# Grouping two matmuls with the rounded weights and two with their remainder in the experts' gate and up products

## What is computed

```python
gate, idx = lax.top_k(aff.T, cap)
xg = xt[idx]
h = jax.nn.silu(jnp.einsum('ecd,edf->ecf', xg, w_gate)) * jnp.einsum('ecd,edf->ecf', xg, w_up)
y = jnp.einsum('ecf,efd->ecd', h, w_down) * gate[..., None].astype(x.dtype)
out = jnp.zeros_like(xt).at[idx.reshape(-1)].add(y.reshape(-1, D))
```

## Time and profile before

| | |
|---|---|
| median of 3 runs | 1766.36 us (1766.05 to 1768.7) |
| the profiled execution: its time | 1767.66 us |
| the profiled execution: first to last instruction (span) | 1765.8 us |
| mean granted TensorE clock | 0.988 of full speed |
| PE matmul, busy | 1717.8 us (97%) |
| PE weight loads, busy | 1554.8 us (88%) |
| DVE, busy | 1192.7 us (68%) |
| ACT, busy | 1074.2 us (61%) |
| POOL, busy | 391.2 us (22%) |

### The profile page before, as it was taken

One profiled execution on the slowest core, in us unless ns is written; L12 is line 12 of the kernel. 1 busy time (PEld: TensorE's weight loads), 2 busy tenths in 40 slices (PEclk: granted clock), 3 DMA queues, 4 the chain that ended last, 5 costly groups with the idle time before them and its releaser, 6 DMA issues.

```text
span 1765.8 us, 30625 instructions
## 1 busy us (share of the span) xinstructions
PE 1717.8 (97%) x10812; PEld 1554.8 (88%) x10812; DVE 1192.7 (68%) x2367; ACT 1074.2 (61%) x2140; POOL 391.2 (22%) x552
## 2 busy tenths in 40 slices
PE   9999999899999989998999999999999999999994
PEld 9789898788888878887999999999999999999994
DVE  4442533488888972147777877787777877778776
ACT  4333333389999983332566756667666666666665
POOL 1322402255555542220110011100110011100112
PEclk9999999899999999998999999999999999999998
DMA  7556645665545742334786787867868678676885
GB/s 237 129 164 196 193 127 152 161 168 156 150 150 145 217 114 107 114 114 166 266 269 247 256 263 237 273 237 256 273 227 274 240 263 279 220 265 251 268 274 220
DMA packets 203488, 367.18 MB, mean 208 GB/s; under 512 B 39055, under 2 KB 64655, under 8 KB 202831
## 3 DMA queue, kind: packets, MB, share of 16 engines
q1 hardware_dynamic: 190268, 320.92, 54.3%
q0 software_dynamic: 13120, 44.96, 9.9%
HBM read 321.67 MB, written 50.45 MB: 211 GB/s over the span
## 4 chain that ended last, share of the span: by engine, by line
PE 48%; DVE 2%; DMA 2%; ACT 1%; POOL 1%; issue 0%; DVEq 0%; SPq 0%; ACTq 0%; POOLq 0%
PE psum L2148 21%; PE psum L2150 10%; PE psum L2167 3%; PE psum L2168 3%; PE psum L2169 3%; PE psum L2170 3%; PE psum L2171 3%; PE psum L2133 1%; DMA own_rows<-x 1%; DMA x<-y_s,index 0%; DVE raw_weights L1848 0%; DMA rows_s<-xn,tokens 0%; DVE weight_parts L1781 0%; ACT xT_e L2012 0%; POOL final_stats L1740 0%
## 5 line engine op out<-in xcount | busy, mean ns | idle before, releaser
L2148 PE MATMUL psum<-x_parts,weight_parts 128*128 128x384 f32 x2048 | 583.6, 359 | 0.0
L2150 PE MATMUL psum<-x_parts,weight_parts 128*128 128x192 f32 x2048 | 512.7, 250 | 0.0
L1781 DVE TENSOR_TENSOR weight_parts<-raw_weights,weight_parts 128x1024 fp32r<-128x1024 f32 x384 | 451.4, 1220 | 69.3 <-ACT weight_parts L1980 69.3
L1980 ACT ACTIVATE weight_parts<-raw_weights 128x1024 fp32r<-128x1024 f32 x384 | 381.8, 1055 | 23.5 <-DMA raw_weights<-in_w_gate 11.0
L2150 PEld LDWEIGHTS psum<-x_parts,weight_parts 128*128 128x128 f32 x2048 | 391.2, 191 | 0.6
L2148 PEld LDWEIGHTS psum<-x_parts,weight_parts 128*128 128x128 f32 x2048 | 384.4, 188 | 0.8
L603 PE MATMUL psum<-x_hi,w_parts 128*128 128x512 f32 x624 | 193.6, 390 | 0.0
L1721 POOL DMA_INDIRECT x<-y_p,index x15 | 24.1, 1609 | 640.4 <-DVE y_s L1843 640.4
L2007 ACT ACTIVATE h_parts<-up_sum 128x192 fp32r<-128x192 f32 x128 | 46.7, 365 | 169.8 <-DVE up_sum L1796 169.6
L1212 PE MATMUL psum<-w_o_parts,mixed_parts 128*128 128x512 f32 x576 | 140.8, 397 | 1.2 <-DVE w_o_parts L1349 1.2
L603 PEld LDWEIGHTS psum<-x_hi,w_parts 128*128 128x128 f32 x624 | 117.1, 188 | 26.9 <-issue 2.6
(11 more groups left out here) (221 smaller groups left out, 3127.9 us busy)
## 6 DMA issues: line engine op xcount, KB each, us to landing
raw_weights<-in_w_gate SPq DMA_DIRECT2D x32, 2048.0 KB, 7.8
raw_weights<-in_w_up SPq DMA_DIRECT2D x32, 2048.0 KB, 8.6
raw_weights<-in_w_down SPq DMA_DIRECT2D x32, 2048.0 KB, 8.9
mixed<-in_w_in SPq DMA_DIRECT2D x96, 256.0 KB, 4.3
q_parts<-q SPq DMA_DIRECT2D x188, 128.0 KB, 3.1
bias_da<-da_rows SPq DMA_DIRECT2D x31, 512.0 KB, 4.4
q<-mixed POOLq DMA_DIRECT2D x96, 128.0 KB, 3.1
mixed<-in_x SPq DMA_DIRECT2D x12, 512.0 KB, 6.9
```

What stands on the lines that cost most here:

```text
L1781: dve.tensor_tensor(part_half(u, 1, half), src, part_half(u, 0, half).bitcast(F32), ALU.subtract).then_inc(split, 1)
L1980: act.activation(part_half(u, 0, half), src, ACT.Copy).then_inc(rounded, 1)
L2148: pe.matmul(out.rearrange("p (h n) -> p h n", h=2), w[:, 0, k, cols], x_parts[:, k, :, :], start=(k == 0), stop=False)
L2150: mm = pe.matmul(out[:, 0:SLOTS], w[:, 1, k, cols], x_parts[:, k, 0, :], start=False, stop=(k == KT - 1))
```

## The change

In `product` the loop over the 8 feature tiles k becomes a loop over 4 pairs of tiles. In each pair the two hi matmuls stand together, then the two lo matmuls. The instructions are the same, with the same operands; the wait for the second half of the first expert's tokens (`x_split`) stays ahead of k = 4.

```diff
-                    for k in range(KT):
-                        if k == HALF_KT and second_half:
+                    for pair in range(0, KT, 2):
+                        if pair == HALF_KT and second_half:
                             pe.wait_ge(x_split, second_half)
-                        pe.matmul(out.rearrange("p (h n) -> p h n", h=2), w[:, 0, k, cols], x_parts[:, k, :, :],
-                                  start=(k == 0), stop=False)
-                        mm = pe.matmul(out[:, 0:SLOTS], w[:, 1, k, cols], x_parts[:, k, 0, :],
-                                       start=False, stop=(k == KT - 1))
+                        for k in (pair, pair + 1):
+                            pe.matmul(out.rearrange("p (h n) -> p h n", h=2), w[:, 0, k, cols], x_parts[:, k, :, :],
+                                      start=(k == 0), stop=False)
+                        for k in (pair, pair + 1):
+                            mm = pe.matmul(out[:, 0:SLOTS], w[:, 1, k, cols], x_parts[:, k, 0, :],
+                                           start=False, stop=(k == KT - 1))
                     return mm
```

## The result

The changed kernel takes a median of 1771.72 us over 20 runs (1769.63 to 1774.54), the kernel before in the same series 1767.72 us (1765.46 to 1769.78): a ratio of **1.0023, 95% interval 1.0017 to 1.0029, 4.0 us slower**. The forecast was 1765.4 us in a range of 1761 to 1770, with 0.07 for slower.

The account below looks back on a forecast made before the run. TensorE's own pace was taken to bound the experts. A group of two hi and two lo was to stay at 568.8 ns; with 1.0 us taken off for the kernel, the forecast was 1765.4 us, range 1761 to 1770.

Parts of the forecast that it names:

- the rival with loads further ahead: In TensorE, the second lo's load is done beneath the second hi; 35.2 ns saved a group, 1730.4 us; chance 0.03.
- The rival with neighbours at their own pace: Two lo in a row step at 93.3 ns; 17.6 ns saved a group, 1748.4 us; chance 0.06.
- no step falls below 110 to 112 ns: In TensorE, one weight load sets a minimum step of 110 to 112 ns, whether 128 columns pass or 16.
- the list for each group: For hi, hi, lo, lo: 173.5, 173.5, 110.9 and 110.9 ns, in sum 568.8, the same as before.
- the order cannot matter: Each matmul in a product covers one equally wide load, so a group takes 568.8 ns in either order.
- The bounds: Time of a group hi, hi, lo, lo: 564.0 to 570.6 ns, or 4.9 us less to 1.8 us more.
- The rival that ended on the other side: Two late loads in a row delay the next hi; 1024 groups lose 20 us, 1787 us; chance 0.07.
- point of decision: Loss per group from which the slower rival counts: 3.4 ns, or 3.5 us (about 0.2%) for the kernel.
- the 16-column run: The router's 16-column matmuls; the first 512-column one after them takes 0.25 us against 0.227, some 0.02 us lost.

Follow-up runs that it names:

- e8: Changed order with lo narrowed from 192 to 128 columns; median 1769.03 us, ratio to before 1.0008.
- e2: Changed order with lo widened from 192 to 256 columns; median 1791.73 us, ratio to before 1.0139.
- e15: Changed kernel, but each expert's first gate product alternates hi and lo as before; median 1765.04 us, ratio to before 0.9989.
- e3: Changed order, but the lo of odd k adds to the second half of the bank; median 1771.41 us, ratio to before 1.0024.
- e5: Alternating order of before with lo widened to hi's 384 columns; median 1893.69 us, ratio to before 1.0717.
- e6: Changed order with lo widened to hi's 384 columns; median 1894.57 us, ratio to before 1.0715.
- e10: Alternating order of before with one group hi, hi, lo, lo at the start of each product; median 1775.59 us, ratio to before 1.0050.
- e13: Alternating order of before with one group hi, hi, lo, lo per expert, in its first gate product; median 1776.79 us, ratio to before 1.0057.
- e14: Alternating order of before, only the first lo of each expert has 256 columns; median 1767.53 us, ratio to before 1.0003.
- e7: Order of before, but each product has one place with two hi and one with two lo, apart; median 1770.17 us, ratio to before 1.0017.
- e4: Each product runs its eight hi, then its eight lo, where before alternates; median 1772.01 us, ratio to before 1.0027.
- e9: Order of before, but each product has two hi in a row mid-product and two lo at its end; median 1775.13 us, ratio to before 1.0043.
- e1: Alternating order of before with lo widened from 192 to 256 columns; median 1785.67 us, ratio to before 1.0108.
- e12: Changed order with lo widened from 192 to 320 columns; median 1848.43 us, ratio to before 1.0463.
- e11: Alternating order of before with lo widened from 192 to 320 columns; median 1845.38 us, ratio to before 1.0444.

## Why the prediction was wrong

**What held.** TensorE's own pace was the only thing that counted; no wait, no other engine and no transfer had a part in it. The load sets the lo step, and only one set of weights is loaded ahead: in the groups every load starts 2 ns or more after the matmul ahead of it, none two matmuls early, and e8's shorter lo holds the array no less. So the rival with loads further ahead fell. The Trainium skill, "TensorE: Matmul & The Clock Gate", section "Back-to-back issue gap", gives a sustained 81 ns for 128 columns and 131 ns for 512. This case does not agree: a lo of 128 columns takes 108 to 112 ns in the changed order too (e8). The rival with neighbours at their own pace fell as well; two lo in a row take 108.3 and 110.9 ns. One reading was too wide, though without effect on the sum: that no step falls below 110 to 112 ns. The transposes behind expert 8, also of 128 columns, stand in the trace of before as

```profile
1335.56 0.80 PE L2133 MATMUL psum<-ident_r,rows_p 128*128 128x128 f32 x8
1336.19 0.46 PE L2167 MATMUL psum<-weight_parts,h_parts 128*128 128x512 f32 x1
```

that is eight steps in 0.63 us, 79 ns each. The floor belongs to the loads of the products, not to every load of 128 columns.

**The step that failed** is the list for each group, two hi of 173.5 ns and two lo of 110.9, with its conclusion that the order cannot matter. Measured, the four are 179.9, 174.3, 108.3 and 110.9 ns: 573.4 in place of 568.8, and the mis-sized term is the first hi. It took a step's length for a property of the step and its neighbour, so that lengths read in other runs could be added up. The runs show that the length of a hi step depends on how the sequence was entered: 176.1, or 179 and 184 ns by turns, in one and the same alternation, 179.9 and 174.3 or 176.6 and 170.8 in one and the same group order. The bounds fell with it: 564.0 to 570.6 ns a group were put together from steps of other sequences, and hold the fast pace (566.6) but not the slow one (573.4) in which the change runs.

**The rival that ended on the other side** had the place right: the first hi after two lo went from 176.1 to 179.9 ns, in record from 358 to 362, and the loss of 4.5 ns a group is above its point of decision, 3.4. Its mechanism was not: it made the lateness of two loads the debt and priced it at 20 us from the 16-column run. The debt comes without late loads (e2), does not grow with them (e8), and is absent in e15 with the same late loads.

**What stays open.** What inside TensorE holds a pace was not found. It is not the columns of PSUM that are written (e3), nor lateness (e2, e8); with steps of one shape there is no sign of it, and there the order of weights and tokens does not matter (e5, e6). Why the 512-column run ahead leads the alternation into its fast pace and the groups into their slow one was only observed, in one trace for each kernel.

## What to carry to other kernels

Where TensorE alternates long and short matmuls, take a step's length only from the same sequence entered in the same way; a sum of steps from elsewhere can be off by up to 2%, here 284.4 ns against 283.3 to 290.1 for the same two matmuls. A reordering that should cost nothing deserves a look at start-to-start times well past the place that was changed, since behind one group of four the next 252 matmuls ran at another pace. Look at every entry, too: in e10, e13 and e14 the first expert did the opposite of the other 15. If a sequence runs slow with no wait in sight, try another way into it, such as one product in another order, before giving the order up.

## What the runs showed that was not expected

- One and the same alternation of 384 and 192 columns runs at 284.4 or 290.1 ns a pair, and one and the same group order at 566.6 or 573.4 ns, and either lasts until something upsets it. In e15's first expert the groups went from the fast pace to the slow one at a single step 0.03 us late.
- The paces stand on a grid. In experts 2 to 16, once steady, a product of 16 matmuls takes 2266.7 ns (e15), 2280.0 (e8), 2286.7 (e7), 2293.3 (the change, e3, e4), 2306.7 (e9), 2313.3 (e10), 2320.0 (e13), 2346.7 (e1), 2373.3 (e2), 2586.7 (e12) or 2773.3 (e5, e6): all whole multiples of 6.67 ns, 340 to 416 of them. Before (2275.6) and e11 (2577.8) come out whole over three products. What sets this grid is not shown.
- In a run of equal steps 384 columns settle at 173.3 ns (e4, e5) and 192 columns at 111.7, the latter being the load. A hi right after a 512-column matmul takes 171.
- Four groups in a product (286.7 ns a pair) cost less than one (289.2).
